# Triangular inversions as quarter products, key products made once, and norms of two mixers moved into the stream

## The reference, cut to what matters

```python
unit_lower = a_mat + jnp.eye(C, dtype=a_mat.dtype)
solve = functools.partial(lax.linalg.triangular_solve, left_side=True, lower=True, unit_diagonal=True)
u = solve(unit_lower, vb)
w = solve(unit_lower, kb * jnp.exp(gc)[..., None])
...
state = (state * w_t[:, :, None, :] + sa[..., None] * b_t[:, :, None, :]
         + v_t[..., None] * k_t[:, :, None, :])
...
yn = ((y - mean) * lax.rsqrt(var + RW_GN_EPS)).reshape(B, S, RW_WIDTH) * ln_w.astype(f32) + ln_b.astype(f32)
y_d = (yn + (bonuses[0] + bonuses[1]).reshape(B, S, RW_WIDTH)) * gate
return jnp.concatenate([y_c.astype(h.dtype), y_d.astype(h.dtype)], axis=-1) @ w_out
```

## Time and profile before

| | us |
|---|---|
| runs | 3040.58, 3043.23, 3050.79 |
| median | 3043.23 |
| profiled execution | 3038.12 |
| its span | 3036.0 |
| even layer, four groups of inversions | 395 to 550 |
| even layer, last tail to output product | 562.91 to 574.01 |
| odd layer, four groups of inversions | 1906 to 2109 |
| odd layer, last tail to output product | 2126.11 to 2143.79 |

### The profile page before, as it was taken

How to read it: one execution, slowest core, us unless ns; L and a number is a source line. 1 busy time by engine, 2 the same in 40 slices (tenths; PEclk the granted TensorE clock), 3 DMA queues, 4 the chain that set the end, 5 groups by cost and what they waited for, 6 DMA issues and landing times.

```text
span 3036.0 us, 45974 instructions
## 1 busy us (share of the span) xinstructions
PE 2929.5 (96%) x19074; PEld 2682.3 (88%) x19074; DVE 1569.0 (52%) x1923; ACT 1271.0 (42%) x1564; POOL 186.2 (6%) x169
## 2 busy tenths in 40 slices
PE   8999999899999999999999997999999999999999
PEld 7999989788998989899898896888888989898897
DVE  4555456565544454544545466543655444544544
ACT  4543322364544534444444444122455434444443
POOL 0000055100000000000000001432000000000000
PEclk9999999999999999999999999888999999999999
DMA  6454300344455555555445550001344555545554
GB/s 255 167 193 181 139 1 1 120 172 153 167 184 191 183 194 188 187 193 181 166 167 180 201 194 18 1 1 56 111 167 139 188 187 182 192 182 194 181 185 149
DMA packets 67918, 462.31 MB, mean 152 GB/s; under 512 B 7007, under 2 KB 10079, under 8 KB 12940
## 3 DMA queue, kind: packets, MB, share of 16 engines
q1 hardware_dynamic: 63680, 449.95, 41.6%
q10 hardware_dynamic: 3500, 5.21, 0.5%
q0 software_dynamic: 544, 4.19, 0.4%
HBM read 457.21 MB, written 5.27 MB: 152 GB/s over the span
## 4 chain that ended last, share of the span: by engine, by line
PE 90%; DVE 6%; ACT 2%; DMA 1%; issue 1%; POOL 0%; SPq 0%; DVEq 0%; ACTq 0%; POOLq 0%
PE bank L406 13%; PE bank L407 13%; PE bank L408 13%; PE bank L381 12%; PE bank L382 12%; PE bank L383 12%; PE bank L1028 3%; PE bank L1012 2%; PE bank L2008 1%; PE bank L1225 1%; PE bank L507 1%; DVE hT_lo L520 1%; DVE split_lo L332 0%; DMA par<-in_small 0%; DMA hwork<-bias_rows 0%
## 5 line engine op out<-in xcount | busy, mean ns | idle before, releaser
L332 DVE TENSOR_TENSOR split_lo<-raw,split_hi 128x1024 fp32r<-128x1024 f32 x840 | 1026.6, 1225 | 1089.8 <-ACT split_hi L325 1088.9
L325 ACT ACTIVATE split_hi<-raw 128x1024 fp32r<-128x1024 f32 x840 | 889.2, 1061 | 1289.3 <-PE bank L408 677.1
L406 PE MATMUL bank<-hT_hi,split_hi 128*128 128x256 f32 x3376 | 957.0, 283 | 10.3 <-issue 4.5
L407 PE MATMUL bank<-hT_lo,split_hi 128*128 128x256 f32 x3376 | 956.1, 283 | 0.0
L408 PE MATMUL bank<-hT_hi,split_lo 128*128 128x256 f32 x3376 | 956.0, 283 | 0.0
L406 PEld LDWEIGHTS bank<-hT_hi,split_hi 128*128 128x128 f32 x3376 | 648.7, 192 | 8.3 <-DVE split_lo L332 3.6
L407 PEld LDWEIGHTS bank<-hT_lo,split_hi 128*128 128x128 f32 x3376 | 648.7, 192 | 5.1 <-issue 4.8
L408 PEld LDWEIGHTS bank<-hT_hi,split_lo 128*128 128x128 f32 x3376 | 648.8, 192 | 0.0
L381 PE MATMUL bank<-split_hi,u_hi 128*128 128x512 f32 x1152 | 449.4, 390 | 0.0
L382 PE MATMUL bank<-split_lo,u_hi 128*128 128x512 f32 x1152 | 448.3, 389 | 0.0
L383 PE MATMUL bank<-split_hi,u_lo 128*128 128x512 f32 x1152 | 448.3, 389 | 0.0
(11 more groups left out here) (393 smaller groups left out, 2356.7 us busy)
## 6 DMA issues: line engine op xcount, KB each, us to landing
raw<-in_stream SPq DMA_DIRECT2D x420, 1024.0 KB, 4.8
work<-in_mem POOLq DMA_DIRECT2D x2, 2048.0 KB, 9.2
bias_rows<-bias_line SPq DMA_DIRECT2D x1, 3072.0 KB, 15.0
hwork<-bias_rows ACTq DMA_DIRECT2D x2, 1536.0 KB, 9.6
x<-in_x SPq DMA_DIRECT2D x1, 2048.0 KB, 9.4
out<-x SPq DMA_DIRECT2D x4, 512.0 KB, 5.0
const<-in_masks SPq DMA_DIRECT2D x1, 1665.5 KB, 12.9
work<-in_wide ACTq DMA_DIRECT2D x1, 1280.0 KB, 5.8
```

What stands on the lines that cost most here:

```text
L325: nc.scalar.activation(split_hi[:, u % SPLIT], raw[:, b % RAW, (u % 2) * UNIT:(u % 2 + 1) * UNIT], ACT.Copy).then_inc(s_hi, 1)
L332: nc.vector.tensor_tensor(split_lo[:, u % SPLIT], raw[:, b % RAW, (u % 2) * UNIT:(u % 2 + 1) * UNIT], f32(split_hi[:, u % SPLIT]), SUB).th ...
L406: nc.tensor.matmul(out, lhsT=w_hi[:, cols], rhs=hT_hi[:, k, :], start=k == 0, stop=False)
L407: nc.tensor.matmul(out, lhsT=w_hi[:, cols], rhs=hT_lo[:, k, :], start=False, stop=False)
```

## The change

An inverse of levels 0 to 5 is block diagonal with two blocks of 64. The change keeps T, Tt and Pm as 64 columns (rows 0 to 63 for the upper block, 64 to 127 for the lower). Levels 1 to 5 are then two products of 64x64 for each matrix, in opposite quarters of the array, into one bank; level 6 is one quarter product of the matrix itself and one with Tt, and needs no mask. ACT copies the two diagonal blocks into a full 128x128 matrix Tf, DVE writes the third block, POOL clears Tf once for each layer.

Beside this: the key by key and query by key products are made for direction 0 alone and serve both directions. The rows of the even output weights are reordered, so that the output product starts with the convolution half, and the transposes of the heads stand behind its third and fourth unit. The odd layer's norm is split: mean and variance a head pair at a time, the affine part, bonus and gate folded on POOL into one factor and one addend (`pool_norm_weights`), and its transposes stand ahead of and inside the first chunk of the output product. The filler products ahead of both output products are gone; four new ones stand ahead of the pairs, whose two row halves now alternate.

```diff
-        def pe_inv_level(pe, group, views, level, between):
-            T, Tt, Pm, MT = views
+        def pe_inv_level(pe, group, views, AT, level, between):
+            T, Tt, Pm, MT, _ = views
             for d in range(2):
-                pe.wait_ge(iv_mt[d], group * LEVELS + level + 1)
                 pe.wait_ge(iv_t, nth(group, level - 1, d))
-                for m in range(4):
-                    i = nc.tensor.matmul(aux[d][:, m * P:(m + 1) * P], lhsT=MT[(group * LEVELS + level) % len(MT)][:, d, m],
-                                         rhs=T[:, d, m], start=True, stop=True)
+                if level < MASKS:
+                    pe.wait_ge(iv_mt[d], group * MASKS + level + 1)
+                    mask = MT[(group * MASKS + level) % len(MT)]
+                    for m in range(4):
+                        for rows in HALVES:
+                            i = nc.tensor.matmul(aux[d][rows, m * HALF:(m + 1) * HALF], lhsT=mask[rows, d, m, rows],
+                                                 rhs=T[rows, d, m, :], start=True, stop=True)
+                else:
+                    left, right = SIDES[d]
+                    for m in range(4):
+                        i = nc.tensor.matmul(aux[d][right, m * HALF:(m + 1) * HALF], lhsT=AT[d][left, m, right],
+                                             rhs=T[left, d, m, :], start=True, stop=True)
                 i.then_inc(iv_p, 1)
...
+                if level == MASKS:
+                    left, right = SIDES[d]
+                    for m in range(4):
+                        i = nc.tensor.matmul(aux[2 + d][left, m * HALF:(m + 1) * HALF], lhsT=Pm[right, d, m, :],
+                                             rhs=Tt[right, d, m, :], start=True, stop=True)
+                    i.then_inc(iv_q, 1)
+                    continue
+                pe.wait_ge(iv_tt, nth(group, level - 1, d, 0, SMALL))
+                    for j in range(2 if level == SMALL else 1):
+                        for rows in HALVES:
+                            lhsT, rhs = ((Tt[rows, d, m, :], side_of(Pm[rows, d, m], level, d == 1)),
+                                         (Pm[rows, d, m, :], side_of(Tt[rows, d, m], level, d == 0)))[j]
+                            at = (4 * j + m) * 32
+                            out = aux[2 + d][rows, at:at + 32].rearrange("p (n s) -> p n s", s=1 << level)
+                            i = nc.tensor.matmul(out, lhsT=lhsT, rhs=rhs, start=True, stop=True)
...
-                    nc.scalar.activation(Pm[:, d], four(aux[d]), ACT.Copy).then_inc(iv_ps, 1)
+                    rows = SIDES[d][1] if level == MASKS else slice(0, P)
+                    nc.scalar.activation(Pm[rows, d], aux[d][rows, 0:4 * HALF].rearrange("p (m n) -> p m n", n=HALF),
+                                         ACT.Copy).then_inc(iv_ps, 1)
+                if level == MASKS:
+                    for d in range(2):
+                        act.wait_ge(iv_t, nth(group, SMALL, d))
+                        for rows in HALVES:
+                            m = nc.scalar.activation(Tf[rows, d, :, rows], Tt[rows, d], ACT.Copy)
+                    m.then_inc(iv_f, 1)
...
+                    if level == MASKS:
+                        left, right = SIDES[d]
+                        nc.vector.tensor_scalar(Tf[left, d, :, right],
+                                                aux[2 + d][left, 0:4 * HALF].rearrange("p (m n) -> p m n", n=HALF),
+                                                -1.0, None, MULT).then_inc(iv_t, 1)
+                        continue
...
-                    for bk, lhsT, rhs in ((b[0], g_col, const_of("causal", 2 * d + 1)), (b[1], b_col, ident),
-                                          (b[2], dn_kT[:, h, tile], dn_kT[:, h, tile]),
-                                          (b[3], dn_kT[:, h, tile], dn_qT[:, h, tile])):
+                    products = [(b[0], g_col, const_of("causal", 2 * d + 1)), (b[1], b_col, ident)]
+                    if d == 0:
+                        products += [(bank[2], dn_kT[:, h, tile], dn_kT[:, h, tile]),
+                                     (bank[3], dn_kT[:, h, tile], dn_qT[:, h, tile])]
+                    for bk, lhsT, rhs in products:
...
-            pe_keep_busy(bank[1], 11)
-            for b in range(4):
-                pe.wait_ge(s_y, b // 2 + 1)
-                for i in range(2):
-                    for t in range(NT):
...
+            def turn_heads(u):
+                if u not in (2, 3):
+                    return
+                pe.wait_ge(s_y, u - 1)
+                for b in range(2 * u - 4, 2 * u - 2):
+                    for i in range(2):
+                        for t in range(NT):
+                            m = nc.tensor.transpose(aux[b][:, (2 * i + t) * P:(2 * i + t + 1) * P],
+                                                    y_tok[:, t, 2 * b + i, :], ident)
+                    m.then_inc(s_yt, 1)
+
+            pe_out_cross(pe, 0, "ev_out", KD, lambda k, t: hT_tile((k + 8) % KD, t),
+                         lambda k: pe.wait_ge(s_yT, k // 2 + 1), turn_heads)
...
+            act.wait_ge(s_qtg, 2 * DN_GROUPS)
+            for b in range(4):
+                nc.scalar.activation(hT_hi[:, 8 + 2 * b:10 + 2 * b, :], yscT[:, 2 * b:2 * b + 2, :], ACT.Copy).then_inc(s_ysp, 1)
             act.wait_ge(s_oms, 1)
             nc.scalar.activation(o_sd, o_ms, ACT.Sqrt).then_inc(s_osd, 1)
+            hi_upto(act, starts["ev_out"][1] + AHEAD + 2)
             act.wait_ge(s_o, 4)
-            nc.scalar.activation(hT_hi[:, 8:16, :], yscT, ACT.Copy).then_inc(s_ysp, 1)
...
+            for b in range(4):
+                dve.wait_ge(s_ysp, b + 1)
+                nc.vector.tensor_tensor(hT_lo[:, 8 + 2 * b:10 + 2 * b, :], yscT[:, 2 * b:2 * b + 2, :],
+                                        f32(hT_hi[:, 8 + 2 * b:10 + 2 * b, :]), SUB).then_inc(s_yT, 1)
...
-            pe_keep_busy(bank[3], 30)
-            pe.wait_ge(s_ry, 1)
...
+            turn_heads(0)
+            pe_out_cross(pe, 1, "od_out", 8, hT_tile, lambda k: pe.wait_ge(s_yT, 9 + k // 2),
+                         lambda u: turn_heads(1) if u == 1 else None)
...
+            if f and d == 0:
+                pe_keep_busy(bank[3], 4)
...
+            for t in range(NT):
+                for j, lhs in enumerate((btl[f % 2], ktl[f % 2])):
+                    for i in range(2):
+                        bk = pair_banks(f, d)[2 * i + t]
+                        rows = slice(64 * i, 64 * i + 64)
...
+            dve_rwkv_norm(dve, 0, 3, 2)
+            for b in range(2):
+                dve.wait_ge(s_ysp, b + 9)
+                nc.vector.tensor_tensor(hT_lo[:, 2 * b:2 * b + 2, :], ycT[:, 2 * b:2 * b + 2, :],
+                                        f32(hT_hi[:, 2 * b:2 * b + 2, :]), SUB).then_inc(s_yT, 1)
             dve_rwkv_out(dve, RW_F - 1)
...
+            dve_rwkv_norm(dve, 3, 1, 3)
```

More of the change, by code:

```diff
@@ L998, in pool_inv_mask @@
             MT = views[3]
-            n = group * LEVELS + level
+            n = group * MASKS + level
             if n >= len(MT):
-                before, its_level = divmod(n - len(MT), LEVELS)
+                before, its_level = divmod(n - len(MT), MASKS)
                 pool.wait_ge(iv_p if its_level else iv_t,
@@ L1039, in pe_inv @@
             for level in range(1, LEVELS):
-                pe_inv_level(pe, group, views, level, between)
+                pe_inv_level(pe, group, views, AT, level, between)
         def act_inv(act, group, views, between):
-            Pm = views[2]
+            _, Tt, Pm, _, Tf = views
             for level in range(1, LEVELS):
@@ L1586, in pool_even @@
                 AT = dn_AT[hp % 2]
-                for level in range(2, LEVELS):
+                for level in range(2, MASKS):
                     for d in range(2):
@@ L2100, in between @@
                         hi_upto(act, starts["od_out"][1] + AHEAD)
+                    if f + 1 == RW_F and level == 5:
+                        act.wait_ge(s_oms, RW_F)
+                        nc.scalar.activation(norm_of(gsd, 0, 3), norm_of(gms, 0, 3), ACT.Sqrt).then_inc(s_osd, 1)
                 act_inv(act, 4 + f, rw_inv[f % 2], between)
@@ L2271, in pool_odd @@
             pool.wait_ge(s_kd, 1)
+            pool.wait_ge(s_rvt, 2)
+            for Tf in rw_Tt:
+                m = pool_clear(Tf)
+            m.then_inc(iv_clear, 1)
             for d in range(2):
@@ L2281, in pool_odd @@
                         pool_inv_mask(pool, 4 + f, AT, rw_inv[f % 2], level, d)
-                for level in range(2, LEVELS):
-                    if level == LEVELS - 1 and f + 1 < RW_F:
+                for level in range(2, MASKS):
+                    if level == MASKS - 1 and f + 1 < RW_F:
                         pool_rwkv_pre(pool, f + 1)
@@ L2286, in pool_odd @@
                         pool_inv_mask(pool, 4 + f, AT, rw_inv[f % 2], level, d)
+                    if f < 2 and level in (2, 3):
+                        pool_norm_weights(pool, 2 * f + level - 2)
```

189 lines of the change are left out of this document (102 added, 87 removed).

## The result

The changed kernel takes 3001.06 us (median of four runs, 2994.96 to 3004.85). The kernel before takes 3041.9 us (median of four, 3024.60 to 3050.79). The ratio is 0.9871, with a 95% interval of 0.9824 to 0.9917. Of the 61 us forecast, about 41 came. The profiled execution took 3001.5 us for a span of 2999.6 us.

What follows compares the result with a forecast made beforehand. TensorE, busy 96% of the span, was taken as the bound, with stage lengths and DVE, ACT and POOL chains setting the groups. 35 + 8 + 5 + 9 + 12 + 22 - 10 - 20 = 61 us, from 3043.2 to 2982 us, range 2940 to 3025.

Steps and rivals of the forecast that it cites:

- my terms without the inversions (5 + 9 + 12 + 22): Gains in us: key products made once 5, even layer's end 9, odd layer's end 12, odd groups' pairs with their clock 22.
- The inversions (35 + 8 - 10 - 20): Both layers' groups: shorter stages gain 35 us, level 6 and border chain 8; switches cost 10, lower clock 20.
- The stages: Levels 1 to 5 of each group: a quarter-product stage takes 1.34 us instead of 1.79, 35 us saved in all.
- The switches: Between quarter and full-array products, about 42 rounds where TensorE is the bound, 0.24 us each: 10 us lost.
- The clock: Quarter products keep less of the array at work: 2.5 us lost in each of eight groups, 20 us, range 0 to 60.
- The rival of 3020 us: Third rival: clock low for two fifths of the groups' remaining 290 us, 58 us lost in place of 20; 8%.
- Pairs: 64-row pairs in three odd groups: filler in the wait and alternating halves mend clock and pace, 22 us gained.
- Key products: Direction 1 no longer repeats them: 1.8 us saved in each of three groups ahead of the border chain, 5 us.
- The ends: Output products start right behind the last tails: 9 us gained in the even layer, 12 us in the odd.
- the first (no overlap): First rival: quarters do not overlap (bank or issue), losing the 35 us and 3 of the 8; 3020 us, 20%.
- The second's 2947 us: Second rival: quarters overlap fully, 0.90 us a stage, and the clock holds, a further 15 and 20 us; 17%.
- The fourth: Rival: quarter work does not hold the clock in all eight groups; gain gone from 162 us at 0.50; 3062 us, 5%.

Runs made afterwards that it cites:

- the old inversions: The changed kernel with inversions, masks and clears as in the kernel before, the rest of the change kept; 2999.6 us, ratio 0.9881 to the kernel before.
- series (1): Bare 64x64 products, 32 in a series, upper and lower half alternating in one bank, put ahead of the odd groups of the changed kernel; 2.01 us.
- the bare series: Changed kernel with bare products replacing 24 fillers ahead of the odd groups; 8 full and 16 quarter products took 5.34 us in eight rounds, 2.95 in one.
- quarter filler: Changed kernel with filler in last groups and tails, each filler product made as two 64x64 products in opposite quarters; 2977.6 us, ratio 0.9816.
- masks first: Changed kernel, but POOL makes the level 5 masks of an odd group before the next group's btl and ktl products; 2977.7 us, ratio 0.9810.
- series (3): Bare 64x64 products, 32 in a series, all in the upper half, put ahead of the odd groups of the changed kernel; 3.87 us.
- series (5): Bare full products of 128x128 by 64 columns, 16 in a series, put ahead of the odd groups of the changed kernel; 3.52 us.
- full filler: Changed kernel with filler products of 128x128 by 256 columns in the last group and last tail of each layer; 2969.3 us, ratio 0.9775.

## Why the prediction was right in range and 19 us off

**Where the miss lies.** The run with the old inversions splits it. By its ratio it gained 36 us, where my terms without the inversions (5 + 9 + 12 + 22) make 48. The inversions (35 + 8 - 10 - 20) were to bring 13 and brought about 3 by the ratios, too little to be measured. So about half of the miss lies in each part. That the total came near 61 is in part luck: larger errors in the stages and in the clock have opposite signs.

**The stages were right in kind and undersized.** I took 1.34 us from one pair of loads at L1916; it was 1.08. The step that failed: the 0.04 us between two neighbouring loads was taken for the spacing of all 32 records. In the quarter stage the records start in pairs, the two of a pair 0.007 us apart and one pair 0.058 us behind the other, so no single spacing gives its length. Counted as the prediction counts (35 us by 0.45), 0.71 would give 55 us. At full clock, even group 2 was 35.9 us, my 36, since idle time grew with it (2.1 to 6.4 us).

**The switches** I had at 0.24 us a round; the tail's items beside a quarter stage grew by 0.19 us, and the stage takes 0.07 us more than half of series (1); the bare series says 0.34. Right in size.

**The clock was the term that failed.** The sum had 20 us for it, from a range of 0 to 60. Against the old inversions the quarters added 114 us at 0.50 (198 less 84), 57 us. I had reasoned from narrow products; even group 2 ran on quarters at 1.00, and quarter filler lifted both tails to 1.00. Quicker stages end sooner and leave TensorE standing for ACT, DVE and POOL: in odd groups 1 and 2 it was idle for 4.4 us a group with the old inversions and 9.7 with the quarters, in group 1 3.9 of it in front of POOL's masks. Idle time alone does not tell which group falls: even group 1 had 4.8 us of it at a mean clock of 0.87, even group 2 6.4 us at 1.00, and why is open. The rival of 3020 us had the size of this loss right; the larger gain in the stages kept the time at 3001.

**The order on POOL was not in the sum at all.** "Where TensorE sets the pace all of it comes through" was said of odd groups 1 to 3 without following POOL's queue through level 5. The mended order gives 18 us by the ratios, 28 by the two profiled spans. This alone is as large as the whole miss, and part of it is the clock of the point above.

**Pairs:** 22 us forecast, 21.9 found where the inversions are the old ones. In the changed kernel odd groups 0 to 2 fell by only 10.1 us, the rest of it eaten by the two points above. The alternating order did what I had priced at 2.9 to 1.9 us: 16 records take 1.93 us (1953.13 to 1955.06, masks first). **Key products:** 1.8 us in each of even groups 1 and 2, as forecast.

**The ends:** forecast 9 and 12 us net. With the old inversions the stretches from tail to output product fell by 11 and 16 us, in the changed kernel by 6.9 and 10.7, because the tails ran at half clock. Some came back: the rest of the program is 12.2 us longer. Its time at 0.50 grew from 37 to 52 us, 7.5 us; its transposes of heads, now inside it, account for 2, and the late waits for 1.4. The filler had also kept the clock for what follows: records of 0.77 us at 2101.31 against 0.50 at 2143.79. I had put that at 2 us; the odd output product ran at 0.50 for its first 5.7 us, which costs 2.9.

**Of the rivals,** the first (no overlap) fell to series (1) and (3). The second's 2947 us is what the quarters reach once masks and the last groups are mended, with a stage of 1.08 us and not its 0.90. The fourth was 61 us off in time, but nearer than its 5% says: from the first product of the groups to the output product, 148 us of the two layers ran at 0.50, against its turning point of 162. What it had wrong is the cause.

**Of the signs:** a stage near 1.3 us did not come, it was 1.08. Group lengths near 36 us held for even group 2 and for group 1 only in kernels with the clock held; 43 us for odd groups held only with the masks first. Both output products start within 1.5 us of the last tail product. At the pairs themselves the low stretches are 6.8 us long, but up to 13.7 us at the borders beside them. One sign of being wrong did show: a clock under 0.8 in odd groups 1 (0.78) and 3 (0.79) and in the last even group (0.75). It was right to point at the clock term.

## What to carry to other kernels

When a last step is dropped from a loop, look at what was hung on "the last step": here a wait on ACT moved ahead of a product that had time for none. When stages get shorter, the waits of the partners and the clock behind them take the gain; read idle time and granted clock of each stretch together, and fill each wait up to its length. Here filler in a wait added nothing to odd groups 0 and 2, while a microsecond of wait in the odd groups went with another of clock. Quarter products go in alternating halves.

## What the runs showed of the hardware

- A float32 product of 64x64 by 64 columns takes 0.063 us in alternating row halves, 0.121 us in one half, a full one 0.220 us. The Trainium skill (TensorE: Matmul & The Clock Gate, The mechanism) says that weight loads overlap with products in flight only for different row groups. The trace agrees in that series (3) takes 1.9 times as long as (1). It does not show the "only": by their records, loads and products of the same rows both run through all of the 3.52 us of series (5).
- Two row halves write one bank without a price in time: 2.01 against 2.02 us.
- A round from full to quarter products and back costs 0.34 us, where each round holds one full and two quarter products.
- Even group 2 ran at 1.00 on quarter products, and quarter filler gave both tails 1.00 as full filler did. Short stages with waits of 0.5 to 1.6 us between them ran at 0.50 for 24 us (even layer) and 34 us (odd layer) on end; with filler in the waits both tails ran at 1.00.
